# A two-block transformer kernel on one core: the first rows' experts, two more places for rows, and queries of two heads at a time

## The reference, cut to what matters

```python
q = (hf @ w_q).reshape(T, PEER_HEADS, 2, PEER_HALF)          # 256 tokens, 8 heads, 2 x 128
s = jnp.einsum('thpd,hpnd->thpn', q, sub_keys)               # 128 scores for each half
sv, si = lax.top_k(s, PEER_TOPK)                             # 16 best of each half
cand = sv[:, :, 0, :, None] + sv[:, :, 1, None, :]           # 16 x 16 sums
cand_idx = si[:, :, 0, :, None] * PEER_NKEYS + si[:, :, 1, None, :]
cv, ci = lax.top_k(cand.reshape(T, PEER_HEADS, 256), PEER_TOPK)
expert = jnp.take_along_axis(cand_idx.reshape(T, PEER_HEADS, 256), ci, axis=-1)
g = jax.nn.softmax(cv, axis=-1)
# for each token: a = gelu(x . u[expert]);  out = sum over its 128 experts of g * a * v[expert]
```

## Time and profile before

| what | value |
|---|---|
| median of 3 runs | 1164.13 us (1163.85 to 1164.34) |
| the profiled execution, its own time | 1164.81 us |
| its span in the trace | 1163.0 us |
| PE, DVE, ACT, POOL busy | 89%, 70%, 36%, 25% of the span |
| gathers by POOL (software queue) | 269.51 MB, 56.0% of the DMA engines' span |

### The profile page before, as it was taken

How to read it: one execution, slowest core, us unless ns; L and a number is a source line. 1 busy time by engine, 2 the same in 40 slices (tenths; PEclk the granted TensorE clock), 3 DMA queues, 4 the chain that set the end, 5 groups by cost and what they waited for, 6 DMA issues and landing times.

```text
span 1163.0 us, 13661 instructions
## 1 busy us (share of the span) xinstructions
PE 1033.2 (89%) x5034; PEld 694.3 (60%) x5034; DVE 814.5 (70%) x1875; ACT 423.1 (36%) x899; POOL 294.1 (25%) x262
## 2 busy tenths in 40 slices
PE   5999999988999886896877778788899999999997
PEld 3798967644555443342333323233389978999986
DVE  6787856777767776888778645545576878888843
ACT  3465713312323222133221211111265666565631
POOL 0000002444454543444544444444000000000000
PEclk9999999999999998998998999999999999999999
DMA  9987694999999999999999999999884344554540
GB/s 377 424 352 312 262 407 180 391 421 421 421 417 422 421 421 422 421 417 421 421 422 421 421 421 421 422 421 422 325 375 181 146 182 150 189 205 176 187 145 36
DMA packets 48343, 390.15 MB, mean 335 GB/s; under 512 B 5515, under 2 KB 6035, under 8 KB 7317
## 3 DMA queue, kind: packets, MB, share of 16 engines
q0 software_dynamic: 37040, 269.51, 56.0%
q1 hardware_dynamic: 11236, 119.77, 26.3%
HBM read 388.20 MB, written 1.06 MB: 335 GB/s over the span
## 4 chain that ended last, share of the span: by engine, by line
PE 53%; DMA 33%; DVE 8%; ACT 3%; issue 2%; POOL 1%; SPq 0%; DVEq 0%; ACTq 0%
DMA ring<-in_uv,idx 30%; PE ps L1510 17%; PE ps L1878 14%; PE ps L2035 5%; PE ps L1535 2%; PE ps L1746 2%; DVE ring L1296 2%; PE ps L1691 2%; PE ps L1963 2%; DMA ring<-in_w_ada 1%; PE ps L1761 1%; DMA ring<-in_w_in 1%; POOL ring L529 1%; DVE ring L928 1%; ACT probT L789 1%
## 5 line engine op out<-in xcount | busy, mean ns | idle before, releaser
L1878 PE MATMUL ps<-ring,probT 128*128 128x512 f32 x1020 | 487.4, 622 | 103.8 <-ACT probT L789 103.7
L1296 DVE CUSTOM_DVE_ANT_0 ring<-h2t,ring 128x1024 f32<-128x1024 f32 x255 | 309.9, 1223 | 184.4 <-DMA ring<-in_uv,idx 182.3
L1878 PEld LDWEIGHTS ps<-ring,probT 128*128 128x128 f32 x1020 | 191.0, 198 | 336.5 <-issue 188.7
L529 POOL DMA_INDIRECT ring<-in_uv,idx x255 | 291.7, 1144 | 339.8 <-PE ps L1878 278.2
L1510 PE MATMUL ps<-util_r,ring_r 128*128 128x256 f32 x1120 | 192.8, 282 | 0.3 <-ACT util L555 0.3
L917 DVE TENSOR_TENSOR ring_r<-ring,ring_r 128x1024 fp32r<-128x1024 f32 (+1 forms) x134 | 155.5, 1204 | 36.0 <-ACT ring_r L551 36.0
L784 ACT ACTIVATE prob<-prob 128x2 f32<-128x2 f32 (+2 forms) x98 | 20.0, 204 | 398.7 <-DVE prob L1296 398.7
L1510 PEld LDWEIGHTS ps<-util_r,ring_r 128*128 128x128 f32 x1120 | 158.1, 188 | 1.3 <-issue 0.7
L551 ACT ACTIVATE ring_r<-ring 128x1024 fp32r<-128x1024 f32 (+1 forms) x134 | 132.0, 1039 | 39.0 <-PE ps L2035 19.1
L1510 PE MATMUL ps<-h_r,ring_r 128*128 128x256 f32 x704 | 125.2, 281 | 0.6 <-DVE util_r L1268 0.6
L789 ACT ACTIVATE probT<-ct,prob 128x128 f32<-128x128 f32 x256 | 85.5, 392 | 86.3 <-DVE prob L1302 83.4
(11 more groups left out here) (225 smaller groups left out, 981.7 us busy)
## 6 DMA issues: line engine op xcount, KB each, us to landing
ring<-in_w_in SPq DMA_DIRECT2D x11, 2048.0 KB, 13.3
ring<-in_w_up SPq DMA_DIRECT2D x11, 2048.0 KB, 8.1
ring<-in_w_ada SPq DMA_DIRECT2D x7, 2048.0 KB, 10.4
ring<-in_w_down SPq DMA_DIRECT2D x6, 2048.0 KB, 8.0
ring<-in_w_ada SPq DMA_DIRECT2D x8, 1024.0 KB, 14.0
ring<-in_w_out SPq DMA_DIRECT2D x4, 2048.0 KB, 8.7
ring<-in_w_q SPq DMA_DIRECT2D x3, 2048.0 KB, 11.6
ring<-in_w_in SPq DMA_DIRECT2D x4, 1024.0 KB, 10.2
```

Of the source, the lines that this page charges most:

```text
L529: e.indirect_dma_start(out=row_buf[n], out_offset=None, in_=uv, in_offset=bass.IndirectOffsetOnAxis(ap=idx[:, tt, k:k + 1], axis=0)).then_inc(
L1296: e.tensor_tensor_reduce(u, h2t[:, tt, :], u, 1.0, 0.0, ALU.mult, ALU.add, av[:, tt, n % 128:n % 128 + 1]).then_inc(*made.put(("dot", n)))
L1878: ins = e.matmul(acc[half][:, :], diag[:, n % 8, :], row_buf[n][:, D + half * 512:D + (half + 1) * 512], start=(k == 0), stop=(k == 127))
```

## The change

The change has four parts.

1. `first_route` takes the place of the first head's route. After the index of row 0 it forms only the 8 x 8 corner of sums of the eight best of each half (which holds the eight largest sums), takes its eight best, picks their indices, and writes those of rows 1 to 7; then it does the rest of the route (the second eight of each half, the 256 sums with the known eight replaced, the next eight, their pick) and writes the indices of rows 8 to 15. POOL waits for the early mark at rows 1 to 7. The scratch memory of the tile 0 routes moves from `area[:, 4096:6144]` to the second half of `h2t`.
2. Two more places: `VALUES_BUF` (`area[:, 3072:5120]`, freed by the last branch product) for row 2 and each ninth or eighth row up to row 44, and `MERGED_BUF` (`util[:, 4096:6144]`, freed by `mixed(1, 1)`) for rows 7 and 16. The rows 1 to 9 thus have places of their own; from row 10 row n waits for the end of row n - 9, from row 25 of row n - 8, from row 52 of row n - 7, and from row 59 all is as before. What shares this memory waits: the copy of queries of heads 6 and 7 for row 44, the copies of scores of tile 1 for row 16, and the two score products of tile 1's first heads move from row 5 to row 30.
3. Queries of two heads at a time: for heads 4 to 7 of tile 0 and 2 to 7 of tile 1 a piece is one matmul of 512 columns with the tokens stationary (`pair_piece`); when all eight are done ACT copies 128 x 512, PE transposes it in four blocks (`pair_turned`), and ACT copies the result. The pieces follow rows 20 to 33, 50 to 63 (tile 0), 26 to 47, 50 to 71 and 74 to 95 (tile 1).
4. PE no longer waits for a row's arrival; the diagonal's mark, which comes after it, is enough.

```diff
-FIRST_BUFS = ((0, 1), (2, 0), (2, 1), (1, 0), (1, 1), (3, 0), (3, 1))
-QUERIES_BUF = (NSLOT, 0)
+QUERIES_BUF, VALUES_BUF, MERGED_BUF = (NSLOT, 0), (NSLOT, 1), (NSLOT, 2)
+FIRST_BUFS = ((0, 1), VALUES_BUF, (2, 0), (2, 1), (1, 0), (1, 1), MERGED_BUF, (3, 0), (3, 1))
+LAST_ROW_OF = {VALUES_BUF: 44, MERGED_BUF: 24}
...
         b = LATER_BUFS[n][0] if n in LATER_BUFS else queue.popleft()
+        while n > LAST_ROW_OF.get(b, n):
+            b = queue.popleft()
...
-    def row(h, tt, k):
-        if tt:
-            return 26 + 78 * (8 * (h - EARLY_HEADS) + k) // 48
-        return k if h == 2 else 8 + 3 * k // 2 if h == 3 else 20 + 15 * (8 * (h - 4) + k) // 8
...
+    row_of_head = {2: lambda k: k, 3: lambda k: 8 + 3 * k // 2}
+    row_of_pair = {(2, 0): lambda k: 20 + 15 * k // 8, (3, 0): lambda k: 50 + 15 * k // 8,
+                   (1, 1): lambda k: 26 + 3 * k, (2, 1): lambda k: 50 + 3 * k, (3, 1): lambda k: 74 + 3 * k}
...
-                pool.wait_ge(made, ("idx", tt, k // 16) if n else "first idx")
+                pool.wait_ge(made, ("idx", tt, k // 16) if n >= 8 else "first idxs" if n else "first idx")
...
+            def pair_rows(c, tt):
+                act.wait_ge(done, ("pair rows", c, tt))
+                act.wait_ge(made, ("gated rows", 2, 1, 1))
+                e.activation(pair_of_rows, bank(("pair rows", c, tt))[:, :], ACT.Copy).then_inc(*acted.put(("pair rows", c, tt)))
...
+                advance(steps, 2)
+                dve.wait_ge(made, (*key, "s", "at", 1))
+                e.tensor_copy(sif[:, 0:2, 0:8], si[:, 0:2, 0:8]).then_inc(*made.put("first si"))
...
+                e.tensor_copy(idx[:, 0, 0:1], ex0).then_inc(*made.put("first idx"))
+                e.tensor_tensor(corner.rearrange("p (a c) -> p a c", a=8),
+                                sv[:, 0, 0:8].unsqueeze(2).broadcast_to([P, 8, 8]),
+                                sv[:, 1, 0:8].unsqueeze(1).broadcast_to([P, 8, 8]), ALU.add).then_inc(*made.put("corner"))
...
+                e.max(cv[:, 0, 0:8], corner).then_inc(*made.put("corner max"))
...
+                e.max_index(ci[:, 0, 0:8], cv[:, 0, 0:8], corner).then_inc(*made.put("corner at"))
...
+                picked("corner", 0, 8)
+                e.tensor_copy(idx[:, 0, 1:8], ex[:, 0, 1:8]).then_inc(*made.put("first idxs"))
+                advance(steps, 3)
...
+                e.match_replace(cand[1], cv[:, 0, 0:8], cand[0], LOWEST).then_inc(*made.put((*key, "rest")))
...
+                picked("second", 8, 16)
+                e.tensor_copy(idx[:, 0, 8:16], ex[:, 0, 8:16]).then_inc(*made.put(("idx", 0, 0)))
...
+                ins = e.matmul(bank(("pair rows", c, tt))[:, :], h_sb[:, k, tile[tt]], w[:, k, :], start=(k == 0),
+                               stop=(k == KD - 1))
...
-                pe.wait_ge(arrived[n], n)
...
-                if n == 5:
+                if n == 30:
                     for h in range(EARLY_HEADS):
                         tile_scores(h, 1)
```

More of the change, by code:

```diff
@@ L101 @@
 ROW_BUFS = row_buffers()
+LEFT_AT = {b: max(n for n, (c, _) in enumerate(ROW_BUFS) if c == b) for b in LAST_ROW_OF}
 def batch_behind(n):
@@ L521, in gpsimd @@
                     h = LATER_BUFS[n][1]
-                    pool.wait_ge(done, ("scores", 7, 1) if h == 7 else ("q", h, 1))
-                elif b == QUERIES_BUF:
+                    pool.wait_ge(done, ("scores", 7, 1) if h == 7 else ("pair rows", h // 2, 1))
+                elif b == MERGED_BUF:
+                    pool.wait_ge(done, ("mix1", 1, 1))
+                elif b in (QUERIES_BUF, VALUES_BUF):
                     pool.wait_ge(done, ("quarter", 39))
@@ L713, in tile_queries @@
                 if h >= EARLY_HEADS:
-                    act.wait_ge(done, ("rows", 0))
+                    act.wait_ge(done, ("rows", LEFT_AT[VALUES_BUF] if h >= 6 else 0))
                 e.activation(Q3[:, 2 * h:2 * h + 2, tile[tt]],
@@ new lines, in first_route @@
+                dve.wait_ge(made, "corner")
+                e.max(cv[:, 0, 0:8], corner).then_inc(*made.put("corner max"))
+                dve.wait_ge(made, "corner max")
+                e.max_index(ci[:, 0, 0:8], cv[:, 0, 0:8], corner).then_inc(*made.put("corner at"))
+                dve.wait_ge(made, "corner at")
+                e.tensor_scalar(ch[:, 0, 0:8, 0], ci[:, 0, 0:8], 3, None, ALU.logical_shift_right).then_inc(
+                    *made.put("corner row"))
+                e.tensor_scalar(ch[:, 0, 0:8, 1], ci[:, 0, 0:8], 7, None, ALU.bitwise_and).then_inc(
+                    *made.put("corner col"))
@@ new lines, in first_route @@
+                dve.wait_ge(made, (*key, "cand"))
+                e.match_replace(cand[1], cv[:, 0, 0:8], cand[0], LOWEST).then_inc(*made.put((*key, "rest")))
+                dve.wait_ge(made, (*key, "rest"))
+                e.max(cv[:, 0, 8:16], cand[1]).then_inc(*made.put((*key, "second")))
+                dve.wait_ge(made, (*key, "second"))
+                e.max_index(ci[:, 0, 8:16], cv[:, 0, 8:16], cand[1]).then_inc(*made.put((*key, "at2")))
+                dve.wait_ge(made, (*key, "at2"))
@@ L1240, in advance @@
                     next(steps, None)
-            routing = (step for group in ROUTES for step in route(*group, area[:, 4096:6144]))
-            advance(routing, 2)
-            first_expert()
-            advance(routing, 12)
+            spare = h2t[:, 1, :]
+            first_route(spare)
+            first_weights = weights(*ROUTES[0])
             rows_added(2, 1)
-            advance(routing, 1)
+            advance(first_weights, 1)
             row_part(2, 1)
             row_diagonal(2, 1)
-            advance(routing, 2)
+            advance(first_weights, 2)
             shifted(1)
-            advance(routing, STEPS_AHEAD - 17)
+            routing = (step for tt, h0, nh in ROUTES[1:] for step in route(tt, h0, nh, area[:, 4096:6144] if tt else spare))
             def row_gain(tt, half):
@@ L1765, in query_piece, with pair_piece, pair_turned @@
                     banks.give(("q", h, tt), acted, ("q", h, tt))
+            def pair_piece(c, tt, k):
+                w = slots[SLOT_OF["q", c]].rearrange("p (k n) -> p k n", k=KD)
+                pe.wait_ge(loaded[SLOT_OF["q", c]], ("q", c))
+                if k == 0:
+                    group(("pair rows", c, tt))
+                pe.wait_ge(made if k >= 4 else acted, ("shifted", tt, k))
+                ins = e.matmul(bank(("pair rows", c, tt))[:, :], h_sb[:, k, tile[tt]], w[:, k, :], start=(k == 0),
+                               stop=(k == KD - 1))
+                if k == KD - 1:
+                    ins.then_inc(*done.put(("pair rows", c, tt)))
+                    banks.give(("pair rows", c, tt), acted, ("pair rows", c, tt))
+            def pair_turned(c, tt):
+                o = group(("pair columns", c, tt))
+                pe.wait_ge(acted, ("pair rows", c, tt))
+                for j in range(4):
+                    ins = e.transpose(o[:, j * P:(j + 1) * P], pair_of_rows[:, j * P:(j + 1) * P], ident)
+                ins.then_inc(*done.put(("pair columns", c, tt)))
+                banks.give(("pair columns", c, tt), acted, ("pair columns", c, tt))
             def tile_queries(h, tt):
@@ L1801, in tile_scores @@
                 pe.wait_ge(loaded[SLOT_OF["keys", 0]], ("keys", 0))
[L1802 removed]
+                pe.wait_ge(acted, ("pair columns", h // 2, tt) if (h // 2, tt) in PAIR_PLAN else ("q", h, tt))
                 for z in range(2):
```

109 lines of the change are left out of this document (86 added, 23 removed).

## The result

The changed kernel takes 1160.46 us (median of 7 runs, 1159.63 to 1160.76), the kernel before, run beside it, 1164.13 (7 runs, 1163.41 to 1164.66): a ratio of 0.997, 95% interval [0.996, 0.9979]. A second measurement beside other kernels gave 1159.59 (5 runs), ratio 0.9955 [0.9942, 0.9969]. The prediction was 1159.7, faster, in a range of 1157.4 to 1163.0. The profiled execution took 1160.76 with a span of 1158.9, against 1164.81 and 1163.0: 4.1 us less.

A forecast was written before the change was run, and what follows sets the result against it. The prediction took the DMA engines' gather plateau to bound the kernel, so only an earlier start helps. Places 4.2 plus moved score products 0.2, all else 0, gave 4.4 us: 1159.7 from a median of 1164.13, range 1157.4 to 1163.0.

The forecast's parts named there:

- all of it reaches row 0 on PE: Start: the residual sum's delay of about 0.85 us, taken as 0.8, passes in full to row 0 on PE.
- The other bound, 0: Start: lower bound of row 0's 0.8 us delay, as head 1's queries on PE held `turned_x1(1)` nearly as long.
- 4.2 and 0.2: Row 13's dot 4.2 us earlier through the places; 0.2 more from moving two score products away from row 5.
- A dip was to be left from about 207 to 215: Start of the row stream: a dip in the DMA rate remains there, while 190 to 195 gets near 400 GB/s.
- only both parts together carry: Start: early experts alone give nothing on the whole; two places alone leave the hole at 190.
- 0 to 2.0 us lost in rows 50 to 58: Pairs: bounds on their loss there, where PE's denser work equals the gathers' pace; 0 was taken.
- the 7.3 said: Row 56's gather: issue to landing shrinks from 8.6 to about 7.3 us, still over 5.6.
- Part 4: PE's dropped arrival wait: the wait never ended last, so 0; bounds 0 and 0.05 us once, at the last row.
- gathers closer to the 6.6 us: Rival, start: row 10 lands 5.6 us after issue, gain 5.9 us, median 1158.2; chance 0.18.
- 6.6 us is the most that a better start can give back: Start: transfer lost against the plateau's 421 GB/s in four windows, together 6.6 us, caps the gain.
- inside the stream nothing but bytes counts: Row stream, 2.52 us a row: the stage can only become shorter by starting the plateau earlier.
- the slower case: Rival: PE's lower clock falls on rows 50 to 58, 4.8 us slower, 1168.9; chance 0.05.

The follow-up runs named there:

- late issue: Changed kernel, but POOL's gathers of rows 1 to 7 wait for the indices of rows 8 to 15; 1162.96 us, ratio to before 0.9988.
- experts only: Changed kernel with the seven old places, neither added place; early route, pairs and no arrival wait stay; 1164.76 us, ratio to before 1.0001.
- places only: Changed kernel with the first head's old route instead of the early one; added places, pairs and no arrival wait stay; 1164.3 us, ratio to before 0.9992.
- heads: Changed kernel with the query pieces of before, one head at a time, instead of pairs; 1158.98 us, ratio to before 0.9953.
- start's order: Changed kernel with the gate's exponential behind the product copies and tile 1's residual sum between the first route's steps; 1159.25 us, ratio to before 0.9954.
- the two best together: Changed kernel with queries a head at a time and the start's order; 1158.86 us, ratio to before 0.9947.
- the cap: Changed kernel with at most four of DVE's routing steps at a batch from row 96 to row 139; 1160.49 us, ratio to before 0.9958.

## Why the prediction was right, and where its steps were off

**Part 1: right in the main, one term wrong.** Row 1's gather was said for 186.8 and stands at 187.21, 2.57 us behind row 0's where 2.5 were worked out. The second half of the residual sum was said for 193.5 and is at 193.77. The step "through the root, `turned_x1(1)` and the queries all of it reaches row 0 on PE" failed: row 0 is at 206.38, earlier than in the earlier trace rows and not 0.8 us later. The other bound, 0, was the better one, though for a reason that the prediction did not see. Before, ACT began its copy of head 1's queries only at 197.25, while the PE group it waits for had ended at 196.26 (194.76 + 1.50); that 1.0 us of lateness ran through `h_sb` into the 1.06 us that PE waits in the earlier trace rows. In the changed kernel ACT's copy starts at 196.63, when PE is ready (192.86 + 3.73 = 196.59). With this term at 0 the sum would have been 5.2 us and not 4.4. The two rows of ACT, before and after:
```profile
197.25 0.38 ACT L715 ACTIVATE area<-ps 128x256 f32<-128x256 f32 x1 [1.96 <-PE ps L1614]
```
```profile
196.63 0.38 ACT L730 ACTIVATE area<-ps 128x256 f32<-128x256 f32 x1 [0.31 <-PE ps L1899]
```

**Part 2: right in its number, one sentence too strong.** Row 10's gather was said for 211.9 and is at 210.70, earlier by what row 0 on PE was. The gain at row 13 was to be 4.2 and 0.2, the dot at 226.7. It stands at 227.10, 3.8 us earlier than before; but it follows DVE's other work there and not its own landing. At row 15, the first that waits for a full gather on both sides, the gain is 4.6; it is 4.3 to 6.0 in the seven profiles in which the gathers of rows 1 to 9 and PE's order at the start are those of the changed kernel. A dip was to be left from about 207 to 215, and one is there from 210 to 220. PE was to run without a pause to about row 30; it first pauses ahead of row 20, at 249.08 (0.61 us). That only both parts together carry is shown for the experts: alone they are worth 0.2 us at row 255 (0.6 with the start taken off), and their time is before's (ratio 1.0001). For the places it is not: alone they lost 0.5 us in one kernel and gained 2.7 in the other (late issue), against 5.0 to 5.7 by both parts. The pairs are in all these kernels and don't hide a gain: at row 15, ahead of the first pair, "experts only" and "places only" are 0.2 and 0.8 us behind before, "late issue" 1.6 ahead.

**Part 3: the size was off.** It was set at 0, with 0 to 2.0 us lost in rows 50 to 58. Those rows lose nothing of the kind: 422 GB/s in 320 to 340 and 10.75 us from row 56's issue (323.06) to its dot (333.81), more than the 7.3 said and than the 8.7 with heads (324.99 to 333.70): the prediction had the sign of this step wrong. By the profiles the pairs cost 0.4 to 1.5 us at row 255, which come up before row 98 and are not tied to the pairs by any row; by the times (1158.98 for heads, 1159.25 to 1159.3 for pairs in the same batch) the cost is not resolved. The new dent at 460 to 480, which the route's own plan makes, was not foreseen at all, and happened to be nearly free.

**Part 4: right,** 0.

**The sum.** 4.4 us were said, 4.1 came in the profile, 3.7 and about 5.4 in the two measurements. Two errors offset each other: the lead at row 255 was 5.0, 0.6 more than said, and 0.9 us were lost at 962 us, where the change touches nothing and the prediction looked for nothing. That the sum came within 0.3 us of the profile is partly luck. Of the rivals, "gathers closer to the 6.6 us" can't be ruled out: it said 5.9 us, and row 15's gain reaches 6.0 in one profile of that start. The 6.9 us with heads are no proof of it, since the lead there is 4.5 at row 40 and 6.8 at row 98. They also break the prediction's sentences that 6.6 us is the most that a better start can give back and that inside the stream nothing but bytes counts: from row 16 to row 98 the same bytes took between 204.4 and 207.7 us. The clock did not fall before 440 us, so the slower case had no ground.

## What to carry to other kernels

Where a stage is bound by transfers, its start has two gates, the first address and the first free place. Here the first alone gave 0.2 us, the second alone 2.7 us at best, both 5.0 to 5.7: find both in the trace before costing one. A kernel that tests one part alone can bring a stall of its own, as "places only" did, so look for it before reading the part's worth off the time. A dip in the mean rate of the DMA engines is not yet a loss; compare the landings on its two sides. And side work spread over an engine by a budget must be looked at for its largest heap in one batch: here the heap of seven steps made PE's input 2.5 us later, though in the end it cost at most 0.4 us.

## What the runs showed of the hardware

- ACT sometimes got PE's result late by the semaphore, though by the profile PE's matmuls had ended. For the copy of head 1's queries it was 0.9 to 1.1 us in before, places only, start's order and the two best together; in these four PE went on to `turned_x1(1)` without a pause. In the other ten PE paused 0.2 to 0.3 us there, and ACT began 0.0 to 0.4 us behind the end. Longer waits are in the two kernels whose POOL issues seven gathers in a row from 192 to 201 us (ACT idle 2.35 and 2.14 us, ended by "remote"). What holds the result back is open: the start's order issues its gathers nearly as the changed kernel does, and PE's ends are modelled in the profile.
- After PE's stand of 3.56 us in places only the granted clock was 0.65 and 0.67 in the next two windows, and the queries cost 10.01 us for 7.31. In the changed kernel row 100 took 3.78 us after a stand of 6.18, with heads 1.98 after 3.23. With the cap it took 3.26 after a stand of only 1.98: there the clock had been 0.77 over 440 to 460 us, so the last stand alone does not tell what a row costs.
- In the plateau rows land every 2.487 us, with longer steps of 3.4 to 3.5 us at nearly the same rows in all kernels (97 or 98, 118 to 122, 139 to 142, 162, 188 to 193, 243 to 247), while the windows' rate stays at 420 to 422. With some smaller ones they make up 5.0 to 8.4 us from row 15 to row 255. What makes them is open.
